# Softmax weights divided on VectorE and turned in transpose mode, and layer two's modulation sums collected inside layer two's block

## Chip, cores and metric

One NeuronCore of one Trainium2 chip. The metric is the device time in microseconds (us) of one execution of the whole program; lower is better.

## The reference, cut to what matters

Two networks of two layers each run one after the other on 256 tokens of width 1024, all in float32. The change touches only the end of the second network, its latent blocks:

```python
for i in range(DEPTH):                               # two layers
    sh1, sc1, g1, sh2, sc2, g2 = split(silu(c) @ w_ada[i] + b_ada[i], 6)
    h = modulate(rmsnorm(x, norm_pre_mix[i]), sh1, sc1)
    p = h @ w_in[i]                                  # q (8 heads), k, v (2 heads), u
    logits = concat([window_scores + mask, context_scores, sink])
    w = softmax(logits)                              # 256 + 256 keys per query and head
    attn = w_loc @ v + w_ctx @ v_ctx
    mix = concat([attn, fourier_mix(u, w_fourier[i])]) @ w_out[i]
    x_mid = x + g1 * rmsnorm(mix, norm_post_mix[i])
    hf = modulate(rmsnorm(x_mid, norm_pre_ffn[i]), sh2, sc2)
    x = x_mid + g2 * rmsnorm((silu(hf @ w_gate[i]) * (hf @ w_up[i])) @ w_down[i], norm_post_ffn[i])
```

## The kernel before, in words

Every engine runs its own program, written out by hand: `@block.tensor`, `@block.scalar`, `@block.vector`, `@block.sync` (the queue of weight loads) and `@block.gpsimd`. They meet at semaphores. The order in each program is the order of its source, and no scheduler moves anything.

The first network and the context stream of the second take the time up to about 2060 us. Then come the latent blocks `block2("l0", 0, "l")` and `block2("l1", 1, "l")`, called one after the other on each engine. The tokens are two tiles of 128 (`t` is 0 or 1). A block runs in this order on TensorE:

- `lifted(p, t)` turns a tile of the normalised rows into the two-bank PSUM tensor HB and waits until VectorE and ScalarE have modulated it into HT; then the input products q0, q1, kv of that tile (`of_tile`), and for both tiles u0 (`by_tokens`).
- Keys and queries are turned by the helper `transposes` (line 441), four 128x128 transposes to a bank.
- The scores of tile 0 (line 995), `channels_dft` (line 961, tiles "mw"), the product u1 (line 453), the scores of tile 1, and `positions_dft` (line 951, tiles "pf").
- Attention for each tile: per head, four matmuls against a diagonal matrix turn the 128x512 exponentials into the tile "pT" and multiply them by the inverse sums (line 1021). VectorE copies pT of even heads to SBUF, ScalarE that of odd heads. `values(c)` (line 1014) multiplies a pair of heads by the values. It stands one pair behind: values(0) follows head 3.
- Between the tiles `fourier` (lines 984 and 985). Then the output product (`out_by_tiles`, line 1081), the gate and up products (lines 1119 and 1137) and the down product (line 1167, tiles "dn").

PSUM banks are dealt in a ring of five (`open_bank`): a tile waits until the tile five places before it has been emptied by the engine named in it, V or A.

On VectorE `scores(t, half)` scales and masks, `maxima(t, ...)` takes the maxima of four heads (line 2554), ScalarE takes the exponentials with their sums, and `diagonals(t, half)` forms 1/sum and one 128x512 product of the identity with it, the four diagonals DG of half the heads (line 2601). The mark "dg" lets TensorE begin those four heads. DG holds only one tile's diagonals, so for tile 1 `diagonals` first waits until tile 0's pT of that half is full.

Layer two's six modulation vectors: while layer one's gate and up products run, VectorE sums weight rows times silu(c) into MQ (`part_of_sum`), of which eight pieces of 128x512 are left whose 128 partitions have still to be added up. TensorE does that at the end of layer one, between the up product and the down product: four products of a matrix of ones with 128x512 pieces for the two gates g1 and g2 (line 1154, tiles "ga"), and sixteen products with a single column of ones for sh2 and sc2 (line 1158, tile "mc"). ScalarE copies them (line 1330). VectorE then forms the modulation columns (`finish_mod`) and both gate rows (`gate_row`, two 128x1024 operations each, with rows of biases and norms that SyncE loads by `load_rows`; the second load stands in the stream of down weights). All of this is for use in layer two.

## Time and profile before

| What | us |
|---|---|
| Three runs | 2774.18, 2768.51, 2772.47 |
| Median | 2772.47 |
| The profiled execution, first to last instruction (its span) | 2769.1 |
| TensorE busy in the span | 1889.1 |
| VectorE busy in the span | 1874.9 |

The profiled execution has no time of its own beside its span. The span lies inside the spread of the three runs, 3.4 us under their median. In the profile PE is TensorE's matmuls, PEld its weight loads, DVE VectorE, ACT ScalarE, SPq the queue of SyncE. Times in the trace count from the span's start. The latent blocks take roughly its last 700 us, layer one to about 2413 us and layer two from there.

### The profile page before, as it was taken

How to read it: one execution, taken by the hardware profiler on the slowest of the kernel's cores; microseconds unless marked ns; L12 is line 12 of the kernel's file. 1: busy time of each engine (PE TensorE's matmuls, PEld its weight loads, DVE VectorE, ACT ScalarE, POOL GpSimd, SP SyncE). 2: the span in 40 equal slices, each digit the busy share in tenths (PEclk: the TensorE clock that was granted, in tenths of full speed). 3: DMA queues.
4: the chain of work that ended last, by engine and by line, in shares of the span. 5: the costliest groups of instructions: out<-in, count | busy, mean ns of one | idle time of the engine just before them, and what ended most of it. 6: DMA issues, size and time to landing. Idle time of an engine off the chain costs nothing.

```text
span 2769.1 us, 24483 instructions
## 1 busy us (share of the span) xinstructions
PE 1889.1 (68%) x8517; PEld 1371.7 (50%) x8517; DVE 1874.9 (68%) x3412; ACT 404.5 (15%) x904; POOL 1083.9 (39%) x1059
## 2 busy tenths in 40 slices
PE   7988444276654363544535546689439999999998
PEld 5786111265443161134333145564237887478873
DVE  2758998889578979988889997676974342242001
ACT  1321001122103020012111010000104100041000
POOL 2004435577256555755566765555640000000000
PEclk8999555596676675967767878889759999999999
DMA  9629999999899999999999989999963693422443
GB/s 342 226 80 375 399 395 400 332 377 378 324 397 404 399 401 401 350 332 405 404 397 389 358 313 394 392 391 409 354 243 107 218 299 125 163 93 92 152 152 121
DMA packets 357626, 850.48 MB, mean 307 GB/s; under 512 B 23832, under 2 KB 147072, under 8 KB 357376
## 3 DMA queue, kind: packets, MB, share of 16 engines
q0 software_dynamic: 148672, 538.17, 50.7%
q1 hardware_dynamic: 208832, 310.76, 32.1%
q8 instruction: 68, 1.11, 0.2%
q14 instruction: 54, 0.44, 0.0%
HBM read 847.79 MB, written 1.05 MB: 307 GB/s over the span
## 4 chain that ended last, share of the span: by engine, by line
PE 37%; DMA 32%; DVE 14%; issue 11%; POOL 3%; ACT 2%; SPq 1%; DVEq 0%; POOLq 0%; ACTq 0%
PE bank L1137 13%; DMA RING<-in_peer_v,EX 7%; PE bank L1167 6%; DMA W<-in_w_ada 5%; DMA W<-in_ada_w 4%; PE bank L453 3%; DMA RING<-in_peer_u,EX 3%; DMA W<-in_w_gate 3%; DMA WORK<-in_peer_u,EX 3%; DMA W<-in_w_up 3%; PE bank L462 2%; POOL RING L1295 2%; PE bank L1081 2%; DVE ACC L2032 2%; DMA WORK<-in_peer_v,EX 2%
## 5 line engine op out<-in xcount | busy, mean ns | idle before, releaser
L1137 PE MATMUL bank<-HT,W 128*128 128x256 f32 x1984 | 457.5, 395 | 59.9 <-DMA W<-in_w_gate 30.8
L1295 POOL DMA_INDIRECT RING<-in_peer_u,EX x343 | 327.4, 955 | 355.9 <-DVE ACC L2014 224.3
L2014 DVE SCALAR_TENSOR_TENSOR ACC<-RING,hrows 128x1024 bf16<-128x1024 f32 x343 | 407.2, 1218 | 86.1 <-DMA RING<-in_peer_u,EX 80.1
L1295 POOL DMA_INDIRECT RING<-in_peer_v,EX x341 | 382.7, 1122 | 197.1 <-issue 76.4
L1137 PEld LDWEIGHTS bank<-HT,W 128*128 128x128 f32 x1984 | 392.7, 199 | 123.9 <-DMA W<-in_w_gate 34.0
L490 PE MATMUL bank<-W,CACT 128*32 128x512 f32 x544 | 117.1, 959 | 200.1 <-DMA W<-in_w_ada 117.3
L1295 POOL DMA_INDIRECT WORK<-in_peer_v,EX x171 | 196.1, 1147 | 103.0 <-DVE hrows L2032 45.7
L1167 PE MATMUL bank<-W,WORK 128*128 128x512 f32 x528 | 230.2, 599 | 2.4 <-DVE WORK L2716 2.4
L1295 POOL DMA_INDIRECT WORK<-in_peer_u,EX x169 | 160.4, 949 | 168.1 <-DVE ACC L2014 145.7
L2014 DVE SCALAR_TENSOR_TENSOR ACC<-WORK,hrows 128x1024 bf16<-128x1024 f32 x169 | 201.4, 1218 | 33.9 <-DMA WORK<-in_peer_u,EX 33.3
L2032 DVE SCALAR_TENSOR_TENSOR ACC<-RING,ACTS,ACC 128x1024 f32<-128x1024 f32 x155 | 198.5, 1281 | 27.1 <-DMA RING<-in_peer_v,EX 26.6
L2032 DVE SCALAR_TENSOR_TENSOR hrows<-RING,ACTS,hrows 128x1024 f32<-128x1024 f32 x154 | 198.1, 1287 | 24.3 <-DMA RING<-in_peer_v,EX 23.1
L2716 DVE TENSOR_TENSOR WORK<-WORK,bank 128x256 f32<-128x256 f32 x66 | 27.2, 420 | 251.9 <-ACT WORK L1725 251.9
L441 PE MATMUL bank<-consts,XN 128*128 128x128 f32 x152 | 32.9, 395 | 228.5 <-DVE XN L2107 99.3
L1167 PEld LDWEIGHTS bank<-W,WORK 128*128 128x128 f32 x528 | 101.2, 192 | 129.8 <-issue 126.6
L744 PE MATMUL bank<-HT,W 128*128 128x128 f32 x832 | 120.6, 315 | 51.0 <-DMA W<-in_peer_wq 28.1
L490 PEld LDWEIGHTS bank<-W,CACT 128*32 128x32 f32 x544 | 14.6, 135 | 264.9 <-DMA W<-in_w_ada 100.3
L1330 ACT ACTIVATE WORK<-bank 128x512 f32<-128x512 f32 (+5 forms) x167 | 87.7, 542 | 394.2 <-PE bank L744 124.5
L744 PEld LDWEIGHTS bank<-HT,W 128*128 128x128 f32 x832 | 117.8, 229 | 54.8 <-DMA W<-in_peer_wq 27.2
L441 PEld LDWEIGHTS bank<-consts,XN 128*128 128x128 f32 x152 | 28.0, 210 | 231.2 <-DVE XN L2107 100.3
L453 PE MATMUL bank<-W,HT 128*128 128x256 f32 x480 | 115.6, 404 | 16.4 <-DMA W<-in_w_in 8.5
L882 PE MATMUL bank<-RING,WORK 128*128 128x512 f32 x108 | 66.4, 746 | 75.1 <-DMA RING<-in_peer_v,EX 75.0
(434 smaller groups left out, 2826.1 us busy)
## 6 DMA issues: line engine op xcount, KB each, us to landing
W<-in_ada_w SPq DMA_DIRECT2D x36, 1024.0 KB, 11.7
W<-in_w_gate SPq DMA_DIRECT2D x33, 1024.0 KB, 7.7
W<-in_w_up SPq DMA_DIRECT2D x33, 1024.0 KB, 5.5
W<-in_w_down SPq DMA_DIRECT2D x33, 1024.0 KB, 5.0
W<-in_w_in SPq DMA_DIRECT2D x32, 1024.0 KB, 16.5
W<-in_w_ada SPq DMA_DIRECT2D x32, 1024.0 KB, 17.2
W<-in_peer_wq SPq DMA_DIRECT2D x24, 1024.0 KB, 18.2
W<-in_w_o SPq DMA_DIRECT2D x10, 1024.0 KB, 15.6
```

Of the source, the lines that this page charges most:

```text
L441: mm = pe.transpose(b[0:rows, j * P:(j + 1) * P], a, ident)
L453: mm = pe.matmul(b[:, t * 256:t * 256 + cols], hT[:, k, t * P:(t + 1) * P], w[:, k, 0:cols], start=(k == 0), stop=(k == K - 1))
L462: mm = pe.matmul(b[:, j * S:(j + 1) * S], w[:, k, j * P:(j + 1) * P], hT[:, k, :], start=(k == 0), stop=(k == DC - 1))
L490: mm = pe.matmul(b[32 * k:32 * k + 32, :], CACT[:, 4 * c + k, :], w[:, k, :], start=(c == 0), stop=(c == 1), skip_group_check=True)
L744: mm = pe.matmul(b[:, at:at + P], w[:, k, at:at + P], HT[:, 4 * c + k, T], start=first, stop=(c == 1 and k == 3), skip_group_check=True)
L882: mm = pe.matmul(bs[hf][:, :], DIAG[:, i, :], SLOT[g % NS][:, hf * 512:(hf + 1) * 512], start=(i == 0), stop=(i == len(picks) - 1))
L1137: mm = pe.matmul(bs[j][:, g * S:(g + 1) * S], w[:, k, j * P:(j + 1) * P], HT[:, k, :], start=(k == 0 and g == 0), stop=(k == DC - 1 and g ...
L1167: mm = pe.matmul(bs[2 * t + hf][:, :], GU[:, 2 * c + k, t * P:(t + 1) * P], w[:, k, hf * 512:(hf + 1) * 512], start=(c == 0 and k == 0), s ...
L1295: gp.indirect_dma_start(SLOT[g % NS], None, rows, bass.IndirectOffsetOnAxis(EX[:, t, k:k + 1], 0))\
L1330: free(name, A(out_, b[:, :] if src is None else src(b), ACT.Copy, scale=scale))
L2014: ve.scalar_tensor_tensor(out=JUNK[:, g % 2, :], in0=SLOT[g % NS], scalar=1.0, in1=HB[:, :], op0=ALU.mult, op1=ALU.mult, accum_out=ACTS[:, ...
L2032: ins = ve.scalar_tensor_tensor(out=acc, in0=SLOT[g % NS], scalar=ACTS[:, k:k + 1], in1=acc, op0=ALU.mult, op1=ALU.add)
```

## The change

In the latent blocks VectorE now divides the exponentials themselves, one operation on 128x512 for each head, in place. The mark "unit" counts single heads. TensorE turns them with `transposes`, the helper used for keys and queries. The diagonals and their buffer DG are gone, and with them the wait of tile 1 for tile 0's pT.

Of the modulation of layer two, the sums for gate g1 (`modulation_gate(0)`) stand in layer two's `lifted`, between the transposes of tile 0 and the wait for their modulation. Those for gate g2 (`modulation_gate(1)`) and the sixteen one-column products stand after `channels_dft`, before u1. ScalarE's copies, VectorE's `gate_row` and `finish_mod`, and the second load of rows move accordingly.

```diff
@@ TensorE
+            def modulation_gate(half):
+                pe.wait_ge(summed, len(BY_VECTOR) // 2)
+                for q in (GATE1, GATE2)[half]:
+                    b = open_bank(("ga", "l1", 1, half, q % 2), "A")
+                    pe.matmul(b[:, :], const("ones"), MQ[q], start=True, stop=True).then_inc(filled, 1)
@@ lifted, after the transposes
+                if (p, t) == ("l1", 0):
+                    modulation_gate(0)
@@ block2
                             channels_dft()
+                            if p == "l1":
+                                modulation_gate(1)
+                                b = open_bank(("mc", p), "A")
+                                for q in SECOND:
+                                    for j in range(4):
+                                        mm = pe.matmul(b[:, 4 * (q - 4) + j:4 * (q - 4) + j + 1], MQ[q][:, j * P:(j + 1) * P],
+                                                       const("ones")[:, 0:1], start=True, stop=True)
+                                mm.then_inc(filled, 1)
                             by_tokens(("u1", p), "A", weight(win[:, :, at["u1"]:at["u1"] + 256]), 256, HT)
+                            if p == "l1":
+                                load_rows(d["b_ada_2"][1][5 * D:6 * D], d["norm_post_ffn_2"][1])
...
-                            pe.wait_ge(mark("dg", p), 2 * t + h // 4 + 1)
-                            b = open_bank(("pT", p, t, h), VA[h % 2])
-                            for k in range(4):
-                                mm = pe.matmul(b[:, k * P:(k + 1) * P], SL[t][:, h, k * P:(k + 1) * P], DG[:, h // 4, h % 4, :],
-                                               start=True, stop=True)
-                            mm.then_inc(filled, 1)
+                            pe.wait_ge(mark("unit", p), t * H2 + h + 1)
+                            transposes(("pT", p, t, h), VA[h % 2], [SL[t][:, h, k * P:(k + 1) * P] for k in range(4)])
@@ ScalarE
                     channels_dft()
+                    if p == "l1":
+                        modulation_gate(1)
+                        copy(("mc", p), CR[:, 0, 16:32], lambda b: b[:, 0:16])
                     exponentials(0, SL[0], 0)
...
                         lower("l1", t)
+                        if t == 0:
+                            modulation_gate(0)
@@ VectorE
+                if p == "l1":
+                    gate_row(p, 1, 0)
                 do(ve.memset(KZN, 0.0))
...
-                        if t:
-                            wait_full(ve, ("pT", p, 0, 4 * half + 3))
                         ve.wait_ge(mark("ex", p), t * H2 + 4 * half + 4)
                         inverse_sums(t, hs)
-                        do(ve.tensor_tensor(DG[:, half, :, :], ident.unsqueeze(1).to_broadcast([P, 4, P]),
-                                            RS8[:, t, hs].unsqueeze(2).to_broadcast([P, 4, P]), ALU.mult), mark("dg", p))
+                        for h in range(hs.start, hs.stop):
+                            do(ve.tensor_scalar(SL[t][:, h, :], SL[t][:, h, :], RS8[:, t, h:h + 1], None, ALU.mult), mark("unit", p))
...
+                    if p == "l1":
+                        finish_mod(p, p, 3, 1, True, 0)
                     for i in range(2):
                         out_part(0, i)
...
                     modulated_tile(1)
+                    if p == "l1":
+                        gate_row(p, 1, 1)
```

The same sums, copies, `finish_mod`, `gate_row` and load of rows are taken out at the end of layer one.

TensorE, tile 0's attention in layer one, the first two heads and the first pair of values. WORK and RING name the memory of the exponentials and of the diagonals, obank the result of `values`. Before:

```order
L1021 MATMUL bank<-RING,WORK 128x128 [waits emptied_by_vector,dg_l0]
L1021 MATMUL bank<-RING,WORK 128x128 x3
L1021 MATMUL bank<-RING,WORK 128x128 [waits emptied_by_scalar,dg_l0]
L1021 MATMUL bank<-RING,WORK 128x128 x3
...
L1014 MATMUL obank<-WORK 64x128 [waits emptied_by_scalar,emptied_by_vector]
```

Now:

```order
L440 MATMUL bank<-consts,WORK 128x128 [waits emptied_by_vector,unit_l0]
L440 MATMUL bank<-consts,WORK 128x128 x3
L440 MATMUL bank<-consts,WORK 128x128 [waits emptied_by_scalar,unit_l0]
L440 MATMUL bank<-consts,WORK 128x128 x3
...
L1032 MATMUL obank<-WORK 64x128 [waits emptied_by_scalar,emptied_by_vector]
```

The places stay. The operand is the identity in the constants in the place of a diagonal, and the line is that of the helper.

TensorE, the turn from the up product to the down product in layer one. Before:

```order
L1137 MATMUL bank<-HT,W 128x256 x15
L1154 MATMUL bank<-ROWT,consts 128x512 [waits emptied_by_vector,modulation_summed]
L1154 MATMUL bank<-ROWT,consts 128x512 [waits emptied_by_vector]
L1154 MATMUL bank<-RING,consts 128x512 [waits emptied_by_vector] x2
L1158 MATMUL bank<-consts,ACC 128x1 [waits emptied_by_vector]
L1158 MATMUL bank<-consts,ACC 128x1 x7
L1158 MATMUL bank<-consts,HN 128x1 x8
L1167 MATMUL bank<-W,WORK 128x512 [waits emptied_by_scalar,emptied_by_vector,w_landed1]
```

Now the same place, then the scores of layer two's tile 0 up to u1:

```order
L1151 MATMUL bank<-HT,W 128x256 x15
L1170 MATMUL bank<-W,WORK 128x512 [waits emptied_by_vector,w_landed1]
...
L969 MATMUL bank<-WORK,consts 128x128 [waits emptied_by_vector]
L969 MATMUL bank<-WORK,consts 128x128 x3
L893 MATMUL bank<-RING,consts 128x512 [waits emptied_by_vector,modulation_summed]
L893 MATMUL bank<-RING,consts 128x512 [waits emptied_by_vector]
L1014 MATMUL bank<-consts,ACC 128x1 [waits emptied_by_vector]
L1014 MATMUL bank<-consts,ACC 128x1 x7
L1014 MATMUL bank<-consts,HN 128x1 x8
L452 MATMUL bank<-W,HT 128x256 [waits emptied_by_scalar,w_landed1]
```

Two of the gate products and all sixteen one-column products have moved from ahead of the down product to ahead of u1. The other two stand in `lifted`.

## Rows read from the trace of the kernel before

**Rows 1.** Page: busy time of the engines, and the chain that ended last.

```profile
PE 1889.1 (68%) x8517; PEld 1371.7 (50%) x8517; DVE 1874.9 (68%) x3412; ACT 404.5 (15%) x904; POOL 1083.9 (39%) x1059
...
PE 37%; DMA 32%; DVE 14%; issue 11%; POOL 3%; ACT 2%; SPq 1%; DVEq 0%; POOLq 0%; ACTq 0%
```

**Rows 2.** Windows: stretch and length, busy us (instructions) per engine, TensorE's granted clock, DMA.

```profile
1630.30:1633.70 3.40, 2.85 (x14) 2.85 (x15) 3.37 (x6) 1.63 (x4) 1.06 (x2) 0.50 0.25 101
1633.80:1636.00 2.20, 0.42 (x4) 0.19 (x2) 2.20 (x5) 2.18 (x6) 1.64 (x2) 1.00 0.84 248
...
2116.00:2144.00 28.00, 27.57 (x275) 24.84 (x273) 10.42 (x20) 12.34 (x26) 0.00 (x0) 1.00 0.05 20
...
2333.60:2340.20 6.60, 6.60 (x13) 3.42 (x13) 2.86 (x5) 1.47 (x2) 0.00 (x0) 0.50 0.01 2
```

**Rows 3.** Groups by form, 2060 to 2170 us: busy us, mean ns of one | idle before.

```profile
L1021 PE MATMUL bank<-RING 128*128 128x128 f32 x64 | 7.8, 278 | 0.0
...
L441 PE MATMUL bank<-consts,WORK 128*128 128x128 f32 x16 | 1.9, 272 | 0.0
```

**Rows 4.** Timeline of tile 0's attention, layer one: start, us, engine, what, count [idle before].

```profile
2114.36 0.69 DVE L2601 TENSOR_TENSOR RING<-consts,RS 128x512 f32<-128x512 f32 x1
2114.97 2.28 DVE L2554 TENSOR_REDUCE MX<-RING 128x4 f32<-128x2048 f32 x1
...
2116.79 3.73 PE L1021 MATMUL bank<-RING,WORK 128*128 128x128 f32 x32
...
2117.88 0.69 DVE L1809 COPY WORK<-bank 128x512 f32<-128x512 f32 x1
...
2128.36 0.70 PE L984 MATMUL bank<-WORK 128*128 128x256 f32 x2
```

**Rows 5.** Timeline of tile 1's attention, layer one.

```profile
2131.92 3.73 PE L1021 MATMUL bank<-RING 128*128 128x128 f32 x32
...
2135.59 0.66 PE L1014 MATMUL obank<-WORK 128*64 128x128 f32 x8
...
2136.61 2.05 PE L1021 MATMUL bank<-RING 128*128 128x128 f32 x16
...
2144.36 10.63 PE L1081 MATMUL bank<-W,HT 128*128 128x256 f32 x48 [0.79 <-DVE HT L2611]
```

**Rows 6.** Instructions of line 2476: times in ns, least, median and most.

```profile
L2476 DVE TENSOR_SCALAR RING<-RING,CACT x1: 479/479/479, 2283.2 to 2283.2; 128x512 f32<-128x512 f32 x1
```

**Rows 7.** Timeline of the turn to the down product, layer one.

```profile
2327.11 1.88 PE L1154 MATMUL bank<-ROWT,consts 128*128 128x512 f32 x4
...
2327.79 0.42 DVE L2716 TENSOR_TENSOR WORK<-WORK,bank 128x256 f32<-128x256 f32 x1 [3.03 <-ACT WORK L1725]
...
2330.54 1.84 PE L1158 MATMUL bank<-consts,ACC 128*128 128x1 f32 x16
...
2332.24 2.41 PE L1158 MATMUL bank<-consts,HN 128*128 128x1 f32 x16
...
2334.51 10.86 PE L1167 MATMUL bank<-W,WORK 128*128 128x512 f32 x18
```

**Rows 8.** Timeline: the same turn in the context stream's block.

```profile
1876.18 75.77 PE L1167 MATMUL bank<-W,WORK 128*128 128x512 f32 x176 [1.20 <-DVE WORK L2716]
```

**Rows 9.** Timeline of the start of layer two.

```profile
2415.76 10.60 PE L908 MATMUL bank<-W,HT 128*128 128x256 f32 x48 [1.71 <-DVE HT L2469]
...
2416.78 1.28 DVE L2699 TENSOR_TENSOR XN<-bank,GA 128x512 f32<-128x512 f32 x2
2416.89 0.20 ACT L1374 ACTIVATE SD<-VE 128x1 f32<-128x1 f32 x1 [1.23 <-DVE VE L2695]
...
2440.25 0.83 DVE L1894 TENSOR_TENSOR WORK<-WORK,consts 128x640 f32<-128x640 f32 x1 [10.43 <-ACT WORK L1330]
```

**Rows 10.** Timeline of layer two, u1 to the first head.

```profile
2456.51 7.07 PE L453 MATMUL bank<-W,HT 128*128 128x256 f32 x32
...
2463.52 0.70 PE L995 MATMUL bank<-WORK 64*128 64x256 f32 x4
...
2474.65 3.73 PE L1021 MATMUL bank<-RING,WORK 128*128 128x128 f32 x32
```

**Rows 11.** Timeline of TensorE about 1630 us: sixteen transposes after an idle stretch.

```profile
1630.85 3.37 PE L441 MATMUL bank<-consts,XN 128*128 128x128 f32 x16 [22.27 <-DVE XN L1856]
```

More of the change, by code:

```diff
@@ L249, in network @@
         SL = (S2_["l"], RING[:, 0:4, :].rearrange("p s n -> p (s n)").rearrange("p (h n) -> p h n", h=H2))
-        DG = RING[:, 4, :].rearrange("p (e h n) -> p e h n", e=2, h=4)
         GU = carve(0, NF * S).rearrange("p (f s) -> p f s", f=NF)
@@ L1176, in block2 @@
                     last_read(mm, 0)
-                    if p == "l0" and c == together - 2:
-                        load_rows(d["b_ada_2"][1][5 * D:6 * D], d["norm_post_ffn_2"][1])
                 held = []
@@ L1611, in gelu, with modulation_gate @@
                 do(A(ACTS[:, :], ACTS[:, :], ACT.Gelu), mark("gelu", p))
+            def modulation_gate(half):
+                for q in (GATE1, GATE2)[half]:
+                    copy(("ga", "l1", 1, half, q % 2), GA[:, GATES["l1", 1][half], (q % 2) * 512:(q % 2 + 1) * 512])
             def block2(p, l, who, kv_only=False):
@@ L1733, in block2 @@
                     return
-                if p == "l0":
-                    for q in GATE1 + GATE2:
-                        copy(("ga", "l1", 1, (q - 8) // 2, q % 2), GA[:, GATES["l1", 1][(q - 8) // 2], (q % 2) * 512:(q % 2 + 1) * 512])
-                    copy(("mc", "l1"), CR[:, 0, 16:32], lambda b: b[:, 0:16])
                 for t in range(NT):
@@ L2592, in scores, with to_unit_sum @@
                         settle()
-                    def diagonals(t, half):
+                    def to_unit_sum(t, half):
                         hs = half_heads[half]
-                        if t:
-                            wait_full(ve, ("pT", p, 0, 4 * half + 3))
                         ve.wait_ge(mark("ex", p), t * H2 + 4 * half + 4)
                         inverse_sums(t, hs)
-                        do(ve.tensor_tensor(DG[:, half, :, :], ident.unsqueeze(1).to_broadcast([P, 4, P]),
-                                            RS8[:, t, hs].unsqueeze(2).to_broadcast([P, 4, P]), ALU.mult), mark("dg", p))
+                        for h in range(hs.start, hs.stop):
+                            do(ve.tensor_scalar(SL[t][:, h, :], SL[t][:, h, :], RS8[:, t, h:h + 1], None, ALU.mult), mark("unit", p))
                     def probabilities(t, heads):
@@ L2615, in block2 @@
                         maxima(0, SL[0], half_heads[half])
-                    diagonals(0, 0)
+                    to_unit_sum(0, 0)
                     for half in range(2):
@@ L2619, in block2 @@
                     maxima(1, SL[1], half_heads[0])
-                    diagonals(0, 1)
+                    to_unit_sum(0, 1)
                     maxima(1, SL[1], half_heads[1])
@@ L2623, in block2 @@
                         probabilities(0, (4 * half, 4 * half + 2))
-                        diagonals(1, half)
+                        to_unit_sum(1, half)
                     values(0)
@@ L2720, in block2 @@
                         yield
-                if p == "l0":
-                    finish_mod("l1", "l1", 3, 1, True, 0)
-                    for half in range(2):
-                        gate_row("l1", 1, half)
                 names = [("dn", p, t, hf) for t in range(NT) for hf in range(2)]
```

11 lines of the change are left out of this document (removed).

## The prediction

> **What bounds the kernel now.** The page comes first. No engine fills the span, and the chain that ended last is shared between TensorE, DMA and VectorE [rows 1]. A share of the whole tells nothing about this change, since it acts only after about 2100 us, so the windows come next. In the attention of layer one, 2116 to 2144 us, TensorE is busy for 27.57 of 28.00 us, VectorE for 10.42, and DMA for a 0.05 share [rows 2]. TensorE's own work is the bound there, and what is taken off it shortens the time. Third, the timelines. At the turn to layer one's down product TensorE runs from the gate sums to the one-column products and on without a gap [rows 7], and from u1 of layer two through the second tile's scores to the first head there is hardly one either [rows 10]. Both ends of the move are on TensorE's path.
>
> **Turning the probabilities.** Instruction counts tell the price. Line 1021 issues 64 instructions for the 32 products of one tile, two for each 128x128 product, in 7.8 us. The helper's sixteen transposes are sixteen instructions in 1.9 us [rows 3]. That is 0.24 us against 0.12 us for a turned block. By the dense stretches, 32 instructions in 3.73 us [rows 4, 5], one instruction is 0.117 us, so each tile loses 32 x 0.117 = 3.7 us of TensorE's work.
>
> The Trainium skill ("TensorE: Matmul & The Clock Gate", Terms) calls the transpose mode four times faster for float32. By it a block would cost 0.06 us and each tile would lose another 1.9 us at most; the two kinds of row in this trace show a factor of two, and the measurement decides.
>
> Tile 1 gets nearly all of it. Its probabilities are divided before it starts. Now four heads take 3.7 us and a pair of values 1.02 us (2135.59 to 2136.61) [rows 5]. After the change four heads take 1.87 us, the next pairs 0.93 us each, the values the same. A head is then full every 0.47 us, and one engine must copy every 0.93 us with copies of 0.69 us on VectorE [rows 4] and less on ScalarE, so the copies keep up. Gain: 3.7 us.
>
> Tile 0 gets less, since VectorE stands close behind. It now forms diagonals in 0.69 us at 2114.36, reduces 2.28 us, does three small operations and copies the first head at 2117.88, 0.5 us after that is full [rows 4]. The new division is four operations of 128x512 with a scalar per partition; the nearest row is 0.48 us each [rows 6], overlapping a little, so 1.7 us for the four. The first copy moves by 1.0 us to 2118.9, the second ends at 2120.3, and TensorE, which has turned four heads by 2118.7, begins values(0) at 2119.7. VectorE then divides four heads of tile 1 (1.7 us, and some 0.4 us for the sums) and copies head 4 from 2122.4 to 2123.1. ScalarE has head 5 at about the same time, after its four exponentials. values(2) can start at 2123.6 and values(3) at 2124.6, and `fourier` starts at 2125.7 and not at 2128.36 [rows 4]. Gain: 2.7 us. The bounds for a tile 0 are 1 us (if the in-place operations cost as much as the 0.69 us of the diagonals) and 3.7 us. The other three divisions stand in stretches where VectorE waits for TensorE or ScalarE; if that cover went, each would cost 1.0 us.
>
> Two layers: 2 x (3.7 + 2.7) = **12.8 us less**. DMA is nearly idle there, so nothing collides, and the output product that follows is TensorE's own work.
>
> **The end of layer one.** The gate sums are eight instructions from 2327.11 to 2330.54, 0.43 us each. The one-column products are 32 from 2330.54 to 2334.51, 3.9 us: 0.11 us each at first and 0.15 later [rows 7]. What is left without them is the wait for VectorE's last product, which ends at 2328.21 [rows 7]. The context stream's block makes the same turn without the sums, and TensorE idles 1.20 us there [rows 8]. The down product therefore starts at about 2328.5 and not at 2334.51: 6.0 us less.
>
> A second part shows only in the clock. After 3 us of one-column products the granted clock goes from 1.00 to 0.50 (2.4 to 1.2 GHz) for 6.6 us [rows 2], and the first 18 instructions of the down product take 10.86 us [rows 7] where 18 x 0.43 = 7.8 us would do at the higher level: 3.1 us. Sum **9.1 us less**. The weights for an earlier down product should be there: DMA already idles at 0.01 where it starts now [rows 2].
>
> **The start of layer two.** The first gate's two products (four instructions, 1.7 us) fill a wait of 1.71 us for the modulation of tile 0 [rows 9]. ScalarE's two copies (0.6 us each) stand ahead of a wait of 1.23 us for VectorE's next statistics [rows 9]. VectorE's `gate_row` (two operations of 1.2 us) stands ahead of a wait of 10.43 us for the kv copy [rows 9]. The banks that q0, q1 and kv take are now those of the down product; VectorE empties the last at 2418.1 [rows 9], before kv asks. SyncE's second load of rows waits for that `gate_row` ahead of the w_out loads, which come later anyway and are not needed before the output product. Cost: 0.1 us. `finish_mod` and the other `gate_row` find VectorE waiting for the output and gate products: nothing. If that last cover went, 2.5 us.
>
> **Ahead of u1.** The second gate's products cost 1.7 us and the one-column products 3.5 (32 x 0.11) to 3.9 us, and nothing hides them. ScalarE's exponentials of tile 0 wait for them too, about 5 us, but they end before the later u1 does. If the clock falls as it does now, u1 pays 3.1 us, together 8.7 us; if it doesn't fall, 5.2 us. A last bound is u1's whole 7.07 us [rows 10] at the lower level, 12.7 us. I take **8.0 us more**, near the row with the same 32 instructions.
>
> **Sum.** -12.8 - 9.1 + 0.1 + 8.0 = -13.8 us. The profiled execution goes from its span of 2769.1 to 2755.3 us. Its span is 3.4 us under the median of the runs; against 2772.5 the forecast is 2758.7 us, -0.50%.
>
> **Rivals.** *The copies or the divisions are the bound.* TensorE's stretches shrink to the pace of the copies, and the divisions run at 0.69 us or more. For it: VectorE is only 0.5 us behind tile 0's first head. Against it: its 10.42 us of 28. The attention then gives 1 us in tile 0 and 2.5 in tile 1, 7 us in all: 2764.5 us.
>
> *The one-column products cost more where they are now.* The lower clock lasts through u1 and part of the scores: +12.7 in place of 8.0, so 2763.4 us. For it: their stretch was the only one after 2100 us where the clock fell. Against it: the dense down product brought it back in 6.6 us.
>
> *The clock falls in the attention itself: slower.* Turning by transposes puts fewer array cycles into the same stretch, with more waits for copies in tile 0. What decides is how long TensorE works at the lower level: each us there costs half a us, so 28 us of it eat the gain of 13.8. The attention of one tile is 7.9 us of TensorE's work after the change, and `fourier` 3.4 us. All of it at 1.2 GHz in both layers is 4 x 7.9 + 2 x 3.4 = 38 us more: 2797 us; half of it 2778 us. Against it: before 1630 us TensorE was idle for 22.27 us at 0.50, then did nothing but sixteen transposes [rows 11], and by 1633.8 the granted clock was 1.00 [rows 2]. Transposes alone brought it up. The Trainium skill ("TensorE: Matmul & The Clock Gate", Part 4: PE-mode transpose) states the contrary, that transpose mode doesn't count as busy for the clock. By that rule the clock would fall in each attention, and this rival would be the forecast; the trace disagrees, so I leave it a small chance.
>
> *The transposes are not cheaper here,* or the path leaves TensorE at once: then only the move is left, -1.0 us, 2771.5 us. The helper's rows speak against it.
>
> **How the numbers follow.** Forecast 0.75; copies or divisions 0.09; costlier one-column products 0.08; clock in the attention 0.05; no cheaper 0.03. The predicted time is the forecast's, 2758.7 us. Low end: tile 0 gives 3.7 us too, 14.9 us, and the clock doesn't fall before u1, 5.2 us: -18.7 us, 2753.8, with the spread of the runs 2752. High end: both milder rivals, 2764.5 and 2763.4, with the same spread: 2766. A measurement of this kernel can tell some 0.2%, 5.5 us, from no change. Faster: the forecast and most of the milder rivals, 0.88. Within: the rest of those and the last rival, 0.07. Slower: 0.05, the clock.
>
> **What would show it.** Each step has its place in the profile of the changed kernel. Heads are 16 instructions in 1.9 us for four, `fourier` starts about 2.7 us earlier after the first head, and the output product 6.4 us earlier. The down product of layer one starts some 1.2 us after the up product, at a granted clock of 1.00. A dip to 0.50 appears after layer two's scores of tile 0, and u1 begins 5.2 to 5.6 us later than now, counted from "mw". The prediction is wrong if the clock shows 0.50 in an attention, if a head's four transposes take 0.9 us, or if the wait for a copy ahead of `values` recurs at each pair of tile 1.

## The result and the profile after

| | before | after |
|---|---|---|
| Median of 4 runs of each, same chip | 2773.32 us | 2758.54 us |
| Lowest and highest | 2768.51, 2775.47 | 2754.95, 2761.14 |
| Span of the profiled execution | 2769.1 | 2756.7 |

The ratio is 0.9948, 95% interval 0.9932 to 0.9965: faster by 0.52%. The profiled execution of the changed kernel took 2758.64 us in all, 1.9 us more than its span.

The page of the changed kernel, busy time and chain, beside [rows 1]:

```profile
PE 1868.5 (68%) x8389; PEld 1349.1 (49%) x8389; DVE 1880.9 (68%) x3436; ACT 404.0 (15%) x904; POOL 1086.2 (39%) x1059
...
PE 35%; DMA 23%; DVE 21%; issue 15%; POOL 4%; ACT 1%; SPq 1%; DVEq 0%; POOLq 0%; ACTq 0%
```

TensorE issues 128 instructions less, 32 for each tile of each layer, and is busy for 20.6 us less. VectorE issues 24 more. The chain's shares moved by several per cent of the span, far more than an edit worth 0.5% can move. They say little here.

**A measure that leaves the first 2100 us out.** The two executions were not alike ahead of the edited code: the first score product of tile 1 in layer one, which stands just ahead of the first edit, starts at 2105.66 us before and at 2110.11 us after. In the thirteen traces of this study it starts between 2100.0 and 2117.6 us. From that product to the end of the span is 663.5 us before and 646.5 us after. I call this stretch the tail. It is 17.0 us shorter, and the early part, 4.45 us longer in this pair by chance, hides a quarter of that from the spans (2769.1 - 2756.7 = 12.4 us).

**Attention of tile 0, layer one,** timeline of TensorE and VectorE after the change (start, us, engine, what, count, idle before), beside [rows 4]:

```profile
2118.81 1.68 DVE L2609 TENSOR_SCALAR WORK<-WORK,RS 128x512 f32<-128x512 f32 x4
2120.40 2.28 DVE L2563 TENSOR_REDUCE MX<-RING 128x4 f32<-128x2048 f32 x1
...
2121.24 1.91 PE L440 MATMUL bank<-consts,WORK 128*128 128x128 f32 x16
2123.93 0.66 PE L1032 MATMUL obank<-WORK 128*64 128x128 f32 x8 [0.78 <-DVE WORK L1816]
...
2123.19 1.28 DVE L1816 COPY WORK<-bank 128x512 f32<-128x512 f32 x2
...
2129.92 0.70 PE L992 MATMUL bank<-WORK 128*128 128x256 f32 x2
```

Read it as a race between the two engines. Four heads are turned in 1.91 us, then TensorE idles 0.78 us for VectorE's copy of pT, which had to stand behind four divisions (1.68 us) and the maxima. First head to `fourier`: 2129.92 - 2121.24 = 8.68 us, against 11.57 us.

**Attention of tile 1, layer one,** TensorE after the change, beside [rows 5]:

```profile
2133.48 1.91 PE L440 MATMUL bank<-consts,RING 128*128 128x128 f32 x16
2135.32 0.66 PE L1032 MATMUL obank<-WORK 128*64 128x128 f32 x8
...
2136.35 1.09 PE L440 MATMUL bank<-consts,RING 128*128 128x128 f32 x8
...
2142.18 4.15 PE L1095 MATMUL bank<-W,HT 128*128 128x256 f32 x18 [0.80 <-DVE HT L2618]
```

No wait stands between the heads and the pairs of values. First head to output product: 8.70 us, against 12.44 us.

**The turn to the down product and the start of layer two,** TensorE after the change, beside [rows 7 and 9]:

```profile
2326.29 19.12 PE L1170 MATMUL bank<-W,WORK 128*128 128x512 f32 x44 [1.20 <-DVE WORK L2727]
...
2401.89 1.04 PE L904 MATMUL hrows<-consts,XN 128*128 128x128 f32 x8
2402.77 1.88 PE L893 MATMUL bank<-ROWT,consts 128*128 128x512 f32 x4
2404.63 10.60 PE L916 MATMUL bank<-W,HT 128*128 128x256 f32 x48
```

The down product now follows a wait of 1.20 us, as in the context stream [rows 8], and its 44 instructions in 19.12 us are 0.43 us each from the start. At the start of layer two the four gate instructions fill the wait of 1.71 us entirely: from the transposes to the input product it is 2404.63 - 2401.89 = 2.74 us, and it was 2.74 us.

**Ahead of u1,** TensorE after the change, beside [rows 10]:

```profile
2444.39 1.16 PE L969 MATMUL bank<-WORK,consts 128*128 128x128 f32 x8 [1.27 <-DVE WORK L2599]
2445.39 1.88 PE L893 MATMUL bank<-RING,consts 128*128 128x512 f32 x4
2447.11 1.84 PE L1014 MATMUL bank<-consts,ACC 128*128 128x1 f32 x16
2448.81 1.93 PE L1014 MATMUL bank<-consts,HN 128*128 128x1 f32 x16
2450.59 7.15 PE L452 MATMUL bank<-W,HT 128*128 128x256 f32 x32
2457.68 0.70 PE L1003 MATMUL bank<-WORK 64*128 64x256 f32 x4
```

And the windows of the same kernel: stretch and length, busy us (instructions) of PE, PEld, DVE, ACT, POOL, granted clock, DMA share and GB/s. They are the attention, the start of the down product, and the one-column products with u1:

```profile
2121.20:2142.20 21.00, 19.43 (x210) 16.75 (x208) 12.37 (x26) 11.44 (x24) 0.00 (x0) 1.00 0.03 12
2326.20:2336.20 10.00, 9.91 (x23) 4.48 (x24) 0.00 (x0) 0.61 (x1) 0.00 (x0) 1.00 0.39 145
...
2447.00:2457.70 10.70, 10.70 (x67) 9.49 (x65) 3.16 (x10) 5.13 (x13) 0.00 (x0) 1.00 0.00 0
```

The clock is at 1.00 in all three. Before, the second "mw" started at 2455.52 us and layer two's first transposes at 2413.02 us (TensorE, before):

```profile
2413.02 1.04 PE L898 MATMUL hrows<-consts,XN 128*128 128x128 f32 x8
...
2455.52 1.16 PE L961 MATMUL bank<-WORK,consts 128*128 128x128 f32 x8 [1.27 <-DVE WORK L2590]
```

u1 now starts 6.20 us after the second "mw" (2450.59 - 2444.39) and started 0.99 us after it [rows 10], so 5.2 us more. In this execution the one-column products did not bring the clock down.

**The account.** Each row is a difference of two starts on TensorE. The stretches between the rows kept their length to 0.02 us, so the rows add up to the tail, to within 0.2 us.

| Stretch | before | after | difference | forecast |
|---|---|---|---|---|
| Tile 0, layer one: first head to `fourier` | 11.57 | 8.68 | -2.9 | -2.7 |
| Tile 1, layer one: first head to output product | 12.44 | 8.70 | -3.7 | -3.7 |
| Output product to down product | 190.15 | 184.11 | -6.0 | -6.0 |
| Down product to layer two's first transposes | 78.51 | 75.60 | -2.9 | -3.1 |
| From there to the second "mw" | 42.50 | 42.50 | 0.0 | +0.1 |
| Second "mw" to tile 1's scores | 8.00 | 13.29 | +5.3 | +8.0 |
| Tile 0, layer two | 11.57 | 8.69 | -2.9 | -2.7 |
| Tile 1, layer two | 12.44 | 8.70 | -3.7 | -3.7 |
| Sum | | | -16.8 | -13.8 |

### The profile page after: what moved, and what is told of

Its sections match the earlier page's. It is cut to its first block, busy times and chain, and to the rows that moved or that the text cites. A ratio compares the mean times of both kernels' runs of the same rounds, so it can differ in the third digit from the quotient of the medians.

```text
span 2756.7 us, 24246 instructions
## 1 busy us (share of the span) xinstructions
PE 1868.5 (68%) x8389; PEld 1349.1 (49%) x8389; DVE 1880.9 (68%) x3436; ACT 404.0 (15%) x904; POOL 1086.2 (39%) x1059
## 4 chain that ended last, share of the span: by engine, by line
PE 35%; DMA 23%; DVE 21%; issue 15%; POOL 4%; ACT 1%; SPq 1%; DVEq 0%; POOLq 0%; ACTq 0%
PE bank L1151 13%; PE bank L1170 8%; DMA RING<-in_peer_v,EX 7%; DMA RING<-in_peer_u,EX 5%; DMA W<-in_w_up 3%; DMA WORK<-in_peer_u,EX 3%; DVE ACC L2021 3%; POOL RING L1296 3%; DMA W<-in_w_gate 3%; PE bank L452 2%; DMA W<-in_ada_w 2%; PE bank L1095 2%; DVE ACC L2039 2%; DVE hrows L2039 2%; PE bank L440 1%
## 5 line engine op out<-in xcount | busy, mean ns | idle before, releaser
L440 PE MATMUL bank<-consts,WORK 128*128 128x128 f32 (+1 forms) x329 | 59.2, 341 | 99.2 <-DVE WORK L2163 37.4
L881 PE MATMUL bank<-RING,WORK 128*128 128x512 f32 x108 | 72.6, 808 | 78.0 <-DMA RING<-in_peer_v,EX 78.0
```

The source lines that it names most:

```text
L440: mm = pe.transpose(b[0:rows, j * P:(j + 1) * P], a, ident)
L881: mm = pe.matmul(bs[hf][:, :], DIAG[:, i, :], SLOT[g % NS][:, hf * 512:(hf + 1) * 512], start=(i == 0), stop=(i == len(picks) - 1))
```

## The experiments

Three questions stood behind them. **Parts:** what do the transposes give by themselves, and what does the move give, whose 9 us at the end of layer one are partly paid back ahead of u1? **Mode or order:** does the attention gain by the transpose mode, or by the diagonals and their wait being gone? **Clock:** does the granted clock decide what the move costs ahead of u1?

### The attention's edit alone

```diff
 before.py
-        if t:
-            wait_full(ve, ("pT", p, 0, 4 * half + 3))
...
-        do(ve.tensor_tensor(DG[:, half, :, :], ident..., RS8[:, t, hs]..., ALU.mult), mark("dg", p))
+        for h in range(hs.start, hs.stop):
+            do(ve.tensor_scalar(SL[t][:, h, :], SL[t][:, h, :], RS8[:, t, h:h + 1], None, ALU.mult), mark("unit", p))
...
-        pe.wait_ge(mark("dg", p), 2 * t + h // 4 + 1)
-        b = open_bank(("pT", p, t, h), VA[h % 2])
-        for k in range(4):
-            mm = pe.matmul(b[:, k * P:(k + 1) * P], SL[t][:, h, k * P:(k + 1) * P], DG[:, h // 4, h % 4, :], ...)
-        mm.then_inc(filled, 1)
+        pe.wait_ge(mark("unit", p), t * H2 + h + 1)
+        transposes(("pT", p, t, h), VA[h % 2], [SL[t][:, h, k * P:(k + 1) * P] for k in range(4)])
```

> The attention of the change (divisions on VectorE, transposes on TensorE) in the kernel before; the modulation sums stay at the end of layer one. The stretch from the first score product of tile 1 in layer one to the end (the tail) was 663.5 us in the trace of before and 646.6 us in that of the change, 16.9 us less. Theory (TensorE's instructions are the bound of the attention, and both parts add up): the tail falls by 6.6 us per layer, 13.2 us, to 650.3 us; layer one's down product still starts behind the sums and shows the clock at 0.50 after the one-column products. Rival (most of the gain comes from the move of the sums, and the divisions give it back): the tail falls by less than 8 us.

2761.56 us, ratio 0.996 (0.9946 to 0.9974). The tail is 650.2 us (the theory said 650.3), 13.3 us under before. At the end of layer one the clock still falls for 6.8 us, as before; TensorE and windows of this kernel:

```profile
2322.41 12.83 PE L1162 MATMUL bank<-W,WORK 128*128 128x512 f32 x23
```

```profile
2110.00:2140.00 30.00, 28.43 (x249) 24.09 (x248) 14.17 (x31) 12.57 (x28) 0.00 (x0) 1.00 0.07 28
2321.10:2327.90 6.80, 6.80 (x15) 3.70 (x15) 2.86 (x5) 1.47 (x2) 0.00 (x0) 0.50 0.00 0
```

The attention's part is worth 13.3 us of the 17.0 and needs nothing of the move. The clock is at 1.00 in the attention here too.

### The move alone

```diff
 after.py
-                            pe.wait_ge(mark("unit", p), t * H2 + h + 1)
-                            transposes(("pT", p, t, h), VA[h % 2], ...)
+                            pe.wait_ge(mark("dg", p), 2 * t + h // 4 + 1)
+                            b = open_bank(("pT", p, t, h), VA[h % 2])
+                            for k in range(4):
+                                mm = pe.matmul(b[...], SL[t][:, h, k * P:(k + 1) * P], DG[:, h // 4, h % 4, :], ...)
...
```

> The move of the modulation sums alone, with the diagonals of before. Theory: the tail falls by 9.1 us at the end of layer one (6.0 of instructions, 3.1 of the clock) and rises by 5.2 us ahead of u1: 3.9 us less, 659.6 us, if the clock does not fall before u1. Rival (where the one-column products stand, the clock falls, and the trace of the change was a lucky one): the clock goes to 0.50 in u1, and the tail falls by some 1 us only, 662.7 us.

2773.21 us, ratio 0.9999 (0.9984 to 1.0014); the tail is 663.1 us, and the rival's number was 662.7. Nothing was won. The same place as in the account, timeline and window:

```profile
2445.33 1.16 PE L970 MATMUL bank<-WORK,consts 128*128 128x128 f32 x8 [1.27 <-DVE WORK L2604]
...
2449.74 2.75 PE L1015 MATMUL bank<-consts,HN 128*128 128x1 f32 x16
2452.36 9.66 PE L453 MATMUL bank<-W,HT 128*128 128x256 f32 x32
2461.95 0.70 PE L1004 MATMUL bank<-WORK 64*128 64x256 f32 x4
```

```profile
2450.70:2457.30 6.60, 6.60 (x21) 5.61 (x22) 0.18 (x2) 4.49 (x11) 0.00 (x0) 0.50 0.00 0
```

From the second "mw" to tile 1's scores it is 16.62 us, 8.6 more than before and not 5.3. The clock was at 0.50 for 6.8 us, over the end of the one-column products and the first part of u1. The move takes the fall away from the down product and can get all of it back here.

### The division early, turned in the matrix mode

```diff
 after.py
-                            transposes(("pT", p, t, h), VA[h % 2], [SL[t][:, h, k * P:(k + 1) * P] for k in range(4)])
+                            b = open_bank(("pT", p, t, h), VA[h % 2])
+                            for k in range(4):
+                                mm = pe.matmul(b[:, k * P:(k + 1) * P], SL[t][:, h, k * P:(k + 1) * P], ident, start=True, stop=True)
+                            mm.then_inc(filled, 1)
```

> The change with one thing undone: the divided probabilities are turned by plain products against the identity and not in transpose mode. Theory (the gain of the attention is the transpose mode's one instruction in place of two): each tile gives its 3.7 us back, tile 0 about 2.9: the tail is 13 us longer than the change's 646.6 us, 660 us. Rival (the gain comes from the diagonals' wait and buffer that are gone): the tail stays within 4 us of 646.6 us.

2771.72 us, ratio 0.9993 (0.9978 to 1.0009); the tail is 661.5 us, and the clock was at 0.50 for 3.4 us where u1 begins. Four heads of tile 1 in this kernel:

```profile
2136.03 3.73 PE L1039 MATMUL bank<-consts,RING 128*128 128x128 f32 x32
```

With the same divisions on VectorE at the same places, the products again take 3.73 us for four heads, and the attention's gain is gone. The theory's 660 us is exceeded by 1.5 us, and 3.4 us at 0.50 cost 1.7 us. Beside the move alone the account closes: that kernel had 663.1 us with 6.8 us at 0.50, this one 661.5 us with 3.4 us, a difference of 1.6 us. The divisions in the diagonals' place, and the wait that went with the diagonals, are worth nothing that these traces show. So the division buys nothing by itself. It is the price for the transpose mode, whose operand is the identity and no diagonal with 1/sum in it, and VectorE pays that price where it is hardly waited for.

### The sums regrouped

The one-column products stand ahead of `channels_dft`, gate g2's sums back between the up and the down product, where the down product waits anyway.

```diff
 after.py
+                if p == "l0":
+                    modulation_gate(1)
                 wd = d["w_down_2"][l]...
...
-                            channels_dft()
                             if p == "l1":
-                                modulation_gate(1)
                                 b = open_bank(("mc", p), "A")
                                 ...
+                            channels_dft()
```

> The change with the sums in two other places: the second gate's two products (1.7 us) stand in the wait of 1.20 us ahead of layer one's down product, and the sixteen one-column products stand before both channels_dft banks and so over the wait of 1.27 us for the second of them. Theory (only what fills a wait of TensorE is free): 1.2 and 1.3 us less than the change, tail 644.1 us. Rival (the clock falls after the one-column products where no dense products stand ahead of them): 2 to 3 us of that are lost again, 646.5 us.

2757.6 us, ratio 0.9938 (0.9914 to 0.9961); the tail is 645.6 us, with 3.4 us at 0.50. The down product starts after the gate sums without an idle stretch in the profile, and the one-column products hide the wait of 1.27 us inside `channels_dft`, whose sixteen instructions now follow each other:

```profile
2447.33 3.02 PE L969 MATMUL bank<-WORK,consts 128*128 128x128 f32 x16
```

The tail lies between the theory's 644.1 us and the rival's 646.5 us. Without the fall, at 1.7 us for 3.4 us, it would be 643.9 us, so what fills a wait was as free as the theory says, and the fall recurs. The intervals of this run and of the change overlap.

### The change again

> The change once more, unaltered. In its first trace the clock stayed at 1.00 through layer two, while in the kernel with the move alone it was at 0.50 for 6.8 us from the end of the one-column products, and for 3.4 us with plain products and with the regrouped sums. Theory (the clock falls about where the one-column products stand in most executions, and the first trace of the change was an exception): 0.50 for 3.4 or 6.8 us at the one-column products, tail 648 to 650 us in place of 646.5. Rival (the change as it stands keeps the clock up): tail 646.5 again. The tail runs from the first score product of tile 1 in layer one to the end; it leaves out the first 2100 us, whose length differs by 11 us over the six traces so far.

2758.29 us, ratio 0.9949 (0.9931 to 0.9966); span 2753.0 us; the tail is 648.2 us. The same program, but now the clock falls for 3.4 us. TensorE and the window:

```profile
2443.44 1.93 PE L1014 MATMUL bank<-consts,HN 128*128 128x1 f32 x16
2445.23 8.84 PE L452 MATMUL bank<-W,HT 128*128 128x256 f32 x32
```

```profile
2445.60:2448.80 3.20, 3.20 (x9) 2.48 (x9) 0.00 (x0) 3.18 (x7) 0.00 (x0) 0.51 0.00 0
```

u1 takes 8.84 us and not 7.15. So the difference to the first trace is no property of the kernel. It varies from one execution to the next, as the theory of this run says.

### The sums in TensorE's waits

Gate g1's sums, `modulation_gate(0)`, stand between the up and the down product of layer one. The one-column products stand in layer two's `lifted`, eight (sixteen instructions) for each tile, where TensorE waits for the modulation. Gate g2's two pieces, here `modulation_gate(2)` and `(3)`, stand ahead of `channels_dft` and behind it.

```diff
 after.py
+                if p == "l0":
+                    modulation_gate(0)
                 wd = d["w_down_2"][l]...
...
-                if (p, t) == ("l1", 0):
-                    modulation_gate(0)
+                if p == "l1":
+                    one_column(t)
...
+                            if p == "l1":
+                                modulation_gate(2)
                             channels_dft()
                             if p == "l1":
-                                modulation_gate(1)
-                                b = open_bank(("mc", p), "A")
-                                ...
+                                modulation_gate(3)
```

> The change with every sum laid over a wait of TensorE: the first gate's two products (1.7 us) ahead of layer one's down product (wait 1.20 us), eight one-column products (1.75 us) in each of layer two's two waits for the modulated tiles (1.71 and 1.75 us), one product of the second gate (0.86 us) between the scores and the first channels_dft bank (wait 1.27 us) and one after the second, where nothing hides it. Theory: 5.2 us ahead of u1 become 0.9, and 0.5 us are added at the down product, 3.8 us less than the change without a fall of its clock: tail 642.7 us; and no fall, since the one-column products stand only where TensorE waited anyway. Rival (the new fillers push back the work behind them: ScalarE's copies, or the banks): tail 645 us or more.

2755.06 us, ratio 0.9933 (0.9916 to 0.995); the tail is 643.7 us, and the clock stays at 1.00 to the last down product. That is 1.0 us above the theory. Timeline of TensorE:

```profile
2415.30 1.84 PE L901 MATMUL bank<-consts,HN 128*128 128x1 f32 x16
...
2441.32 1.12 PE L893 MATMUL bank<-RING,consts 128*128 128x512 f32 x2
2443.84 2.02 PE L980 MATMUL bank<-WORK,consts 128*128 128x128 f32 x16 [1.39 <-DVE WORK L2611]
```

Sixteen one-column instructions at a time vanish in `lifted`'s waits of 1.7 us, and the clock doesn't fall. The missing 1.0 us stands in the last two rows. In the change the first bank of `channels_dft` runs ahead of the wait for VectorE's scores and the second behind it (1.27 us). Here the piece of g2 has taken the last bank that was free ahead of the wait, so the wait, 1.39 us, comes before both banks of `channels_dft`. The piece has only changed places with work that stood there already.

### The one-column products among u1's

```diff
 after.py
-                                for q in SECOND:
-                                    for j in range(4):
-...
-                            by_tokens(("u1", p), "A", weight(win[:, :, at["u1"]:at["u1"] + 256]), 256, HT)
+                                for i in range(16):
+                                    last = pe.matmul(b1[...], HT[:, k, ...], w[:, k, :], ...)
+                                    if i < 15:
+                                        for n in range(i, i + 1) if i else (0, 15):
+                                            mm = pe.matmul(b[:, n:n + 1], MQ[4 + n // 4][...], const("ones")[:, 0:1], start=True, stop=True)
```

> The change with its sixteen one-column products (3.5 us) spread among the sixteen dense products of u1, one behind each. The count of instructions is the same. Theory (the clock falls when a stretch holds hardly any dense columns, and dense products among them keep it up): no fall, tail 646.5 us, as in the change's first trace. Rival (the fall depends on the total of work in the neighbourhood, or on the moment alone): 0.50 shows for 3.4 us or more near u1, tail 648 us or more.

2763.53 us, ratio 0.9964 (0.9952 to 0.9976); the tail is 652.9 us. The theory's number is missed by 6.4 us, and the rival's is met. TensorE, VectorE and ScalarE in layer two:

```profile
2456.11 0.70 PE L1003 MATMUL bank<-WORK 64*128 64x256 f32 x4
...
2462.79 1.22 PE L1003 MATMUL bank<-WORK 64*128 64x256 f32 x4 [4.69 <-DVE RING L2608]
```

```profile
2460.23 0.16 DVE L2582 TENSOR_TENSOR RS<-SUM,SE 128x4 f32<-128x4 f32 x1 [13.55 <-ACT WORK L1672]
```

```profile
2455.68 0.18 ACT L1340 ACTIVATE CR<-bank 128x16 f32<-128x16 f32 x1 [9.34 <-PE bank L1020]
```

The clock held through u1, as the theory has it, and u1 with the one-column products took 10.6 us (2456.11 less 2445.53). The loss is elsewhere. ScalarE's copy of the one-column bank stands ahead of tile 0's exponentials. That bank is now full only near the end of u1, so ScalarE idles 9.34 us. VectorE waits 13.55 us for the exponentials ahead of its first division. It has tile 1's scores to empty behind that, and TensorE finds no empty bank for 4.69 us. Within that idle stretch, at 2461.3 us, the clock falls for 6.8 us. So far this is only read from the trace; a run below tests it.

### The one-column products twice

```diff
 after.py
-                                for q in SECOND:
+                                for q in SECOND + SECOND:
```

> The change with the sixteen one-column products done twice over: 3.5 us more of instructions. Theory (a long stretch of one-column products brings the clock down): 0.50 shows within the longer stretch and part of u1 runs at it: tail 646.5 + 3.5 + 2 to 4, 652 to 654 us. Rival (chance alone decides): no fall, 650.0 us.

One run, 2769.92 us; the tail is 656.7 us, above both numbers expected. The clock was at 0.50 for 13.7 us:

```profile
2449.95 2.79 PE L1014 MATMUL bank<-consts,HN 128*128 128x1 f32 x16
2452.61 3.55 PE L1014 MATMUL bank<-consts,ACC 128*128 128x1 f32 x16
2456.02 3.55 PE L1014 MATMUL bank<-consts,HN 128*128 128x1 f32 x16
2459.44 9.62 PE L452 MATMUL bank<-W,HT 128*128 128x256 f32 x32
```

Sixteen instructions take 1.84 us at the higher level and 3.55 us at the lower. In this trace the clock fell within the one-column products, stayed down through the rest of them and came back only under u1. It is one trace, and the fall differs from one execution to the next; but no other fall in any tail of this study is longer than 6.8 us. The tail holds the cost of the added products too, so the fall is read from the granted clock and not from the tail alone.

### Three more, on one chip: the cause of the wait, and the best version

The first is the version among u1's with ScalarE's copy moved behind the exponentials:

```diff
-                        copy(("mc", p), CR[:, 0, 16:32], lambda b: b[:, 0:16])
                         exponentials(0, SL[0], 0)
+                        copy(("mc", p), CR[:, 0, 16:32], lambda b: b[:, 0:16])
```

> As the run with the one-column products among u1's, but ScalarE copies their bank after tile 0's exponentials instead of ahead of them. Theory (ScalarE's order made the wait of 4.69 us ahead of tile 1's scores: the copy stood ahead of the exponentials and its bank was full only at u1's end): that wait falls to below 1 us, the clock stays at 1.00 there, and from tile 1's first score product in layer one to the end of the span it takes 645 to 647 us, against 652.9 with the early copy. Rival (banks or VectorE's maxima hold TensorE, not ScalarE's order): the wait stays above 3 us and the stretch above 650 us.

2755.82 us, ratio 0.9943 (0.9925 to 0.996); the tail is 646.5 us. TensorE and ScalarE:

```profile
2454.22 0.70 PE L1003 MATMUL bank<-WORK 64*128 64x256 f32 x4
...
2456.44 0.70 PE L1003 MATMUL bank<-WORK 64*128 64x256 f32 x4 [0.22 <-DVE RING L2609]
```

```profile
2444.46 1.28 ACT L1670 ACT_TABLE_LOAD   x1
...
2453.79 0.18 ACT L1340 ACTIVATE CR<-bank 128x16 f32<-128x16 f32 x1 [5.01 <-PE bank L1020]
```

The wait of 4.69 us is 0.22 us, the clock stays at 1.00 and 6.4 us come back. One line of ScalarE's order was the whole of it. The tail is no shorter than that of the change where its clock holds: laid among u1's, the one-column products still cost their length.

The second is the version with the sums in TensorE's waits, the third the change itself:

> The version with the sums placed in TensorE's waits again, beside the change itself in the same call. Theory: it is faster than the change by what it saves after tile 1's first score product, 643.7 us against 646.5 to 648.2, so by 3 to 4 us, 0.1 to 0.2%, and its ratio to before is 0.993 to 0.9945. Rival: chance in the first 2100 us hides it, and both ratios agree within 0.05%.

> The change itself, as the measure for the two runs beside it. Ratio to before 0.995; 646.5 to 648.5 us after tile 1's first score product in layer one; the granted clock at 0.50 for 0 to 3.4 us ahead of u1.

| | median of 6 | ratio to before | tail | clock at 0.50 around u1's start |
|---|---|---|---|---|
| sums in the waits | 2751.48 | 0.9926 (0.9909 to 0.9942) | 643.7 | 0 |
| the change | 2759.34 | 0.9948 (0.9928 to 0.9968) | 649.9 | 6.8 us |

The change's tail, 649.9 us, is above what I expected, since its clock fell for 6.8 us this time:

```profile
2456.33 2.74 PE L1014 MATMUL bank<-consts,HN 128*128 128x1 f32 x16
2458.93 9.68 PE L452 MATMUL bank<-W,HT 128*128 128x256 f32 x32
```

```profile
2457.50:2464.10 6.60, 6.60 (x20) 5.61 (x20) 0.37 (x3) 4.49 (x11) 0.00 (x0) 0.50 0.00 0
```

The version with the sums in the waits beats before, and in both comparisons it has a lower median than the change, by 3.2 and by 7.9 us. In the second I expected 3 to 4 us and a ratio of 0.993 to 0.9945. The change's tail was 6.2 us longer there, with 3.4 us of that from its clock. The tail of the version in the waits was 643.7 us both times, and the change's was never under 646.5. The intervals of the ratios still overlap, so the times alone don't settle an advantage. The tails show one of 2.8 to 6.2 us, in two traces against three.

## Why the prediction was right, point by point

- **What bounds.** TensorE's own work bounds the attention. In the changed kernel it is busy for 19.43 of 21.00 us there. The wait that appeared in tile 0 is 0.78 us (1.0 in the working), and there is none between the pairs of tile 1.
- **Turning the probabilities, -12.8 us.** The mechanism and the size were right. The trace gives 2 x (2.9 + 3.7) = 13.2 us, the run of this part alone 13.3 us. The factor of two between the modes, read from instruction counts [rows 3], held: 1.91 us for four heads against 3.73 us. The run in the matrix mode ties the gain to the mode. The race of tile 0 came out to within 0.3 us at both steps that were compared: values(0) started 2.69 us after the first head (2.9 in the working), `fourier` 8.68 us (8.9).
- **The division's cost.** Priced at 1.7 us for four from one row of 0.48 us [rows 6]; it took 1.68 us.
- **End of layer one, -9.1 us.** Measured -6.0 for the instructions and -2.9 for the clock. That the clock falls there without the move is seen in two traces (before and the attention's edit alone), for 6.8 us in both. The wait of 1.20 us from the context stream [rows 8] came out to the digit.
- **Start of layer two, +0.1 us.** Measured 0.0.
- **Ahead of u1, +8.0 us: the term that was mis-sized.** The trace measured +5.3. The bounds were right and the choice between them was not: the step takes one value from "the row with the same 32 instructions", as though one trace settled it. In three traces of the same program it cost 5.3, 7.0 and 8.6 us (the second from 2439.02 to 2454.00, the third from 2451.91 to 2468.55, less 8.00 each), with the clock at 0.50 for 0, 3.4 and 6.8 us. The two ends are the working's own two cases, 5.2 and 8.7 us; what it lacked was that one kernel shows both. A chance for each would have led to about 7 us. "A dip to 0.50 appears" was wrong for the first trace and right for two others.
- **The sum.** -13.8 us for the profiled execution; the tail gives -17.0 there, -15.3 and -13.6 in the two further traces. The forecast is inside these. The medians gave -14.8 us, and -14.8 and -14.4 us in the two further comparisons. That the median, 2758.54 us, met the forecast of 2758.7 us to 0.2 us is luck: the interval of the ratio reaches some 4.6 us to either side, and in the profiled execution one term was off by 2.7 us. Its span, 2756.7 us against the forecast of 2755.3, looks close for the same reason: 4.45 us of chance ahead of the edit stood against some 3 us by which the tail came out better.
- **The rivals.** *Copies or divisions:* not seen, no wait recurs at the pairs of tile 1. *Costlier one-column products:* not seen. With the gate sums beside them they cost up to 8.6 us, never the 12.7 of that rival. Issued twice over they went past it (15.5 us, 2445.53 to 2468.99 less 8.00), with 13.7 us at the lower level. *The clock falls in the attention:* in none of the ten traces that turn by transposes. In the tails every fall before the last down product ends stands at one-column products, just behind them, or in the idle stretch of 4.69 us. *Not cheaper:* refuted by the rows.
- **The prediction's argument from [rows 11].** The attention alone can't show that transposes hold the clock up, since products with the values make up about half of it. The transposes after 22.27 us of idle can, and the other traces have the same place. In three of the thirteen (before, the change again, the one-column products among u1's) the clock rose when TensorE had done nothing but these transposes since the idle stretch; in the change again it rose at 1633.0 us, 1.0 us ahead of the next product:

```profile
1629.60:1632.90 3.30, 2.81 (x14) 2.41 (x12) 3.30 (x7) 2.95 (x7) 2.07 (x3) 0.50 0.29 76
1633.10:1633.90 0.80, 0.00 (x0) 0.00 (x0) 0.80 (x3) 0.78 (x3) 0.54 (x1) 1.00 0.85 318
```

In the other ten it was still at 0.50 when the next products began. So transposes alone can bring the clock up here, and don't in most executions. The rule of the Trainium skill ("TensorE: Matmul & The Clock Gate", Part 4: PE-mode transpose), that transpose mode doesn't count as busy for the clock, is contradicted by the three, for float32.

What the move is worth follows from the same numbers. It saves 9.0 us at the end of layer one and costs 5.3 to 8.6 us in the traces of the change, so a net -3.7 to -0.4 us. The trace of the move alone met the small end (-0.3 us). The whole change against the attention alone, 0.9948 or 0.9949 against 0.996, can't be told apart by time.

Open: why the clock falls in one execution and not in the next, with the same instructions. No run here settles it.

## What to carry to other kernels

Split a change's trace at the last point that it can't have touched, and add up differences of starts from there: with some 0.2% of chance in the time, stretches of a few us are still read to a tenth. Where a factor is folded into a product (here 1/sum into the matrix that turns), ask whether an idle engine can apply it beforehand and free the product for a cheaper mode. Work that is moved off a path still lands on some path: moved into a wait, it costs only what is longer than the wait, unless other work ran there already; moved between two dense products, it costs its full length, and it may take the clock with it. And when a product moves, look at the emptying engine's order too: a copy that waits there for a later bank holds up everything behind it.

## What the runs showed of the hardware

- A block of sixteen products with one column (32 instructions, 3.5 us in all) can cost the clock. In the change it left the granted clock at 1.00 in one trace, and the clock went to 0.50 (1.2 GHz) for 3.4 and for 6.8 us in two others. Each further 3.4 us at the lower level cost 1.7 us: the tails are 646.5, 648.2 and 649.9 us. Over all traces with one such block, in either place, the clock fell at it or just behind it in seven of eight; with 64 instructions, in the one trace, for 13.7 us. The same 32, split between two waits with dense products around them, or laid singly among u1's, brought it down in none of four traces (in one of them it fell later, within the idle stretch of 4.69 us).
- Sixteen transposes alone, after 22.27 us of idle, had the clock back at 1.00 ahead of the next product in three of thirteen traces [rows 11].
- VectorE's in-place division of 128x512 (a product with 1/sum, one scalar per partition) takes 0.42 us each in a row of four (1.68 us); the product with broadcast operands that formed the diagonals took 0.69 us for the same size [rows 4]. Four whole heads are divided for 1.0 us more than their four diagonals had cost.
- Up to the edited code two executions of the same program differ by up to 13 us (2104.7 and 2117.6 us at tile 1's scores in two traces of the change).
